# One decoder step on one core: the identity loaded first, dummy products, and the first product group ordered by terms and token halves

## The reference, cut to what matters

```python
def decoder_layer(h, p, attn_fn, conv_prev, lw):
    z = h @ lw['w_in']                       # (tokens x 1024) @ (1024 x 6400)
    q, k, v, c_b, c_c, c_h, g_a, g_c = jnp.split(z, IN_SPLITS, axis=-1)
    attn, new_k, new_v = attn_fn(q, k, v, lw['attn_sinks'])
    conv, new_conv = short_conv(c_c * c_h, conv_prev, lw['conv_w'])
    merged = (sigmoid(g_a) * (attn @ lw['w_attn_out'])
              + sigmoid(g_c) * (c_b * conv @ lw['w_conv_out']))
    h = layer_norm(DN_ALPHA * h + merged @ lw['w_o'], lw['ln1_g'], lw['ln1_b'])
    eidx, gw = route(x2, lw['w_router'], lw['router_bias'])
    ffn = swiglu(shared) + routed_experts(x2, eidx, gw, ...)
    ...
    return layer_norm(DN_ALPHA * h + ffn + ple, lw['ln2_g'], lw['ln2_b'])
```

## Time and profile before

| what | us |
|---|---|
| median of 3 runs (1264.17 to 1265.15) | 1264.87 |
| span of the profiled execution | 1265.4 |
| PE busy in the profiled execution | 1227.0 (97%) |
| first transpose starts | 7.09 |
| first product starts | 14.96 |
| group 1 starts | 28.32 |

### The profile page before, as it was taken

How to read it: one execution, slowest core, us unless ns; L and a number is a source line. 1 busy time by engine, 2 the same in 40 slices (tenths; PEclk the granted TensorE clock), 3 DMA queues, 4 the chain that set the end, 5 groups by cost and what they waited for, 6 DMA issues and landing times.

```text
span 1265.4 us, 23325 instructions
## 1 busy us (share of the span) xinstructions
PE 1227.0 (97%) x8776; PEld 974.0 (77%) x8777; DVE 497.9 (39%) x1103; ACT 306.3 (24%) x560; POOL 159.8 (13%) x228
## 2 busy tenths in 40 slices
PE   7999999999999999999899999999999999999977
PEld 7988879999999999998899666556555566666643
DVE  4456574423453433566886112112112221111137
ACT  4344453322221222316012111111111111111121
POOL 0200000000000000004336121111111121211100
PEclk9999999999999999999999999999999999999999
DMA  9312122322223232606337999999999999999986
GB/s 279 103 37 67 34 68 51 80 71 79 89 68 100 67 109 76 211 21 208 141 115 305 420 419 419 421 421 419 420 421 419 420 421 418 420 421 421 421 351 264
DMA packets 98656, 307.31 MB, mean 243 GB/s; under 512 B 11244, under 2 KB 62404, under 8 KB 72840
## 3 DMA queue, kind: packets, MB, share of 16 engines
q1 hardware_dynamic: 85332, 275.20, 56.2%
q0 software_dynamic: 12304, 28.60, 5.8%
q10 hardware_dynamic: 948, 2.50, 0.6%
HBM read 294.45 MB, written 26.94 MB: 254 GB/s over the span
## 4 chain that ended last, share of the span: by engine, by line
PE 55%; DMA 37%; DVE 5%; issue 1%; DVEq 1%; ACT 0%; SPq 0%; POOL 0%; ACTq 0%; POOLq 0%
DMA w_exp<-in_w_e_down_dram 35%; PE proj L1051 32%; PE proj L1243 4%; PE proj L1384 3%; PE att L1454 2%; PE proj L1473 2%; PE att L1165 2%; PE att L1127 1%; DMA fold<-expert_rows 1%; PE att L1252 1%; PE proj L1338 1%; PE att L1178 1%; PE proj L1368 1%; PE proj L1077 1%; DVE res L2124 1%
## 5 line engine op out<-in xcount | busy, mean ns | idle before, releaser
L1454 PE MATMUL att<-w_exp,xt 128*64 128x256 f32 x2560 | 286.3, 380 | 2.7 <-DMA w_exp<-in_w_e_up_dram 2.1
L1454 PEld LDWEIGHTS att<-w_exp,xt 128*64 128x64 f32 x2560 | 207.6, 137 | 90.2 <-issue 27.5
L1051 PE MATMUL proj<-h_hi,w_hi 128*128 128x288 f32 x768 | 171.1, 304 | 0.0
L1051 PE MATMUL proj<-h_hi,w_lo 128*128 128x288 f32 x768 | 164.2, 295 | 0.0
L1051 PE MATMUL proj<-h_lo,w_hi 128*128 128x288 f32 x768 | 164.0, 295 | 0.0
L1473 PE MATMUL proj<-w_exp,ht_e 128*64 128x512 f32 x640 | 146.1, 597 | 9.6 <-DMA w_exp<-in_w_e_down_dram 4.9
L1051 PEld LDWEIGHTS proj<-h_hi,w_hi 128*128 128x128 f32 x768 | 122.0, 188 | 16.2 <-issue 15.2
L1051 PEld LDWEIGHTS proj<-h_lo,w_hi 128*128 128x128 f32 x768 | 123.5, 188 | 0.0
L1051 PEld LDWEIGHTS proj<-h_hi,w_lo 128*128 128x128 f32 x768 | 123.4, 188 | 0.0
L468 DVE TENSOR_TENSOR w_lo<-w_raw,w_hi 128x2048 fp32r<-128x2048 f32 x33 | 75.6, 2291 | 91.9 <-ACT w_hi L458 86.8
L1473 PEld LDWEIGHTS proj<-w_exp,ht_e 128*64 128x64 f32 x640 | 50.4, 136 | 77.7 <-issue 76.0
(11 more groups left out here) (384 smaller groups left out, 1810.8 us busy)
## 6 DMA issues: line engine op xcount, KB each, us to landing
w_exp<-in_w_e_gate_dram SPq DMA_DIRECT2D x64, 1024.0 KB, 16.9
w_exp<-in_w_e_up_dram SPq DMA_DIRECT2D x64, 1024.0 KB, 17.0
w_exp<-in_w_e_down_dram SPq DMA_DIRECT2D x64, 1024.0 KB, 17.1
w_raw<-in_w_in_dram SPq DMA_DIRECT2D x21, 1024.0 KB
part<-expert_rows SPq DMA_DIRECT2D x8, 1536.0 KB, 21.2
w_raw<-in_w_in_dram SPq DMA_DIRECT2D x8, 512.0 KB
w_raw<-in_w_attn_out_dram SPq DMA_DIRECT2D x8, 512.0 KB
w_raw<-in_w_conv_out_dram SPq DMA_DIRECT2D x4, 1024.0 KB
```

The source lines that it names most:

```text
L1051: last = nc.tensor.matmul(proj[:, 2 * i + a, 0:HALF], lhs, x[:, c, a * HALF:(a + 1) * HALF], start=(c == 0 and n == 0), stop=(c == KC - 1 ...
L1454: last = nc.tensor.matmul(att[e * SLOT:(e + 1) * SLOT, m, 0:FF], xt[:, c, e * SLOT:(e + 1) * SLOT], weights[e][:, c, :], start=(c == 0), s ...
```

## The change

Four things change, all before group 1.

- ACT's queue issues `ident` first and tile 0 second.
- PE, as soon as `zeroed` is 2, does 11 products of the cleared head of `k_t` with itself (128 x 128, FP32) into bank 3 of `att`. Nothing reads them.
- In ACT's stream the split of group 0 stands behind the fourth copy, no longer behind the sixth.
- PE's products of group 0 are ordered by term and token half, and the last four quads stand between them: six quads, `hi*hi` of half 0 (16 products), four quads, `w_hi*h_lo` of half 0, `hi*hi` of half 1, `w_hi*h_lo` of half 1 (16 each), and last the 32 with `w_lo`. Count and sizes of transposes and products are as before.

```diff
+N_WARM = 11
         def _(act):
+            act.dma_start(ident[:, :], const1[:, 0:P]).then_inc(ld_x, 16)
             act.dma_start(x_tok[:, 0, :], xp[:, 0, :]).then_inc(tile_in[0], 16)
-            act.dma_start(ident[:, :], const1[:, 0:P]).then_inc(ld_x, 16)
...
-                if n == 5:
+                if n == 3:
                     split_hi(act, Step(0))
...
+            pe.wait_ge(zeroed, 2)
+            for _ in range(N_WARM):
+                nc.tensor.matmul(att[:, 3, 0:P], k_t[:, 0:WIN], k_t[:, 0:WIN], start=True, stop=True)
...
             pe.wait_ge(ld_x, 16)
+            token_quads(0, 6)
             pe.wait_ge(hi_done, 1)
+            pe.wait_ge(x_hi, 6)
+            for i in range(2):
+                first_products(0, 0, i)
+            token_quads(6, len(QUADS))
+            pe.wait_ge(x_lo, 6)
+            for i in range(2):
+                first_products(1, 0, i)
+            pe.wait_ge(x_hi, len(QUADS))
+            for i in range(2):
+                first_products(0, 1, i)
             pe.wait_ge(x_lo, len(QUADS))
+            for i in range(2):
+                first_products(1, 1, i)
             pe.wait_ge(w_ready, 1)
             for i in range(2):
+                for a in range(2):
+                    last = first_products(2, a, i)
                 last.then_inc(mm_ready[i], 1)
...
-            pe.wait_ge(zeroed, 2)
             pe.wait_ge(kv_tok_ready, 1)
```

More of the change, by code:

```diff
@@ L1060, in group @@
                         chunk(g, i, c, src_hi, src_lo)
-            pe.wait_ge(ld_x, 16)
[L1063 to L1078, removed]
-            pe.wait_ge(hi_done, 1)
[L1081 to L1085, removed]
+            pe.wait_ge(zeroed, 2)
@@ new lines, in _, with token_quads @@
+            for _ in range(N_WARM):
+                nc.tensor.matmul(att[:, 3, 0:P], k_t[:, 0:WIN], k_t[:, 0:WIN], start=True, stop=True)
+            def token_quads(first, last_n):
+                for n in range(first, last_n):
+                    t, c = QUADS[n]
+                    pe.wait_ge(tile_in[t], 16)
+                    if n >= 4:
+                        pe.wait_ge(x_lo, n - 3)
+                    w = ntok(t)
+                    for j in range(4):
+                        k = 4 * c + j
+                        last = nc.tensor.transpose(att[:, n % 4, j * P:j * P + w], x_tok[0:w, t, k * P:(k + 1) * P],
+                                                   ident[0:w, 0:w])
+                    last.then_inc(tr_x, 1)
@@ new lines, in first_products @@
+            def first_products(n, a, i):
+                w, x = ((w_hi, h_hi), (w_hi, h_lo), (w_lo, h_hi))[n]
+                for c in range(KC):
+                    lhs = w[:, 0, :].rearrange("p (c n) -> p c n", c=KC)[:, c, i * P:(i + 1) * P]
+                    last = nc.tensor.matmul(proj[:, 2 * i + a, 0:HALF], lhs, x[:, c, a * HALF:(a + 1) * HALF],
+                                            start=(c == 0 and n == 0), stop=(c == KC - 1 and n == 2))
+                return last
+            pe.wait_ge(ld_x, 16)
```

## The result

| | before | after |
|---|---|---|
| median us (range) | 1265.15 (1263.82 to 1267.24) | 1268.0 (1265.3 to 1270.02) |
| ratio, 95% interval | | 1.0017 (1.001 to 1.0024) |
| first product of group 0 | 14.96 | 13.57 |
| group 1 starts | 28.32 | 29.44 |

The ratio compares runs on the same chip; 0.17% of 1265 us is 2.1 us. The kernel became a little slower, by less than the 0.2% that counts as a difference here. The first product starts 1.39 us earlier and group 1 starts 1.12 us later: 2.5 us are lost between the two.

A forecast was written before the change was run, and what follows sets the result against it. PE's opening was taken to bound the kernel through group 1's start; +0.1 us for the new order plus 1.85 for low-clock products gave 1264.87 + 1.95 = 1266.8 us, range 1264.0 to 1268.0.

The forecast's parts named there:

- A: Main forecast: group 0's first products run at the low clock, +1.95 us (up to +2.75), 1266.8; chance 0.50.
- B: Rival: clock up and staying up when group 0's products start, despite 2 us idle; +0.1 to -0.7 us; chance 0.32.
- The bound and the lever: Opening before group 1: a microsecond PE wins or loses there moves the expert-weight loads and reaches the end nearly whole.
- The clock decides the sign: Before group 0's products: PE idles 2.0 us (2.9 if clock risen), then products cost 0.238 us instead of 0.133.
- Size of the loss: Group 0's first products: low clock for 4.2 to 6.0 us, costing 1.85 to 2.65 us.
- the fast branch: Opening's transposes at 0.11 us each: first product at 13.4 instead of 14.25, group 1 at 27.6, 0.7 us earlier.
- the uncovered transposes: Between group 0's products: sixteen transposes formerly hidden in ACT's split now cost 1.4 us.
- The dummies' length: Start of PE's stream: 11 dummy products start at 1.1, take 0.22 us apiece and end near 3.6, costing nothing.
- Tile 0's landing: Second load in ACT's queue: tile 0 lands at 6.6 us, between 5.2 and 7.0, without gain reaching the products.
- rival D: Opening: tile 0, now second, lands at 7.0 and PE starts as before; 1265 to 1266.8 us; chance 0.08.
- The stop for `w_lo`: PE's wait within group 0, 0.5 us before, goes: DVE ends `w_lo` at 21.7, its products come after 24.
- Rival C: Group 0's load shares DMA engines with tiles 0 to 3 and lands late; +3.7 us, 1268.6; chance 0.10.

The follow-up runs named there:

- e3: The changed kernel with eight dummy products added in PE's idle gap before the first products; median 1264.15 us, ratio 0.9996 to the kernel before.
- e7: The changed kernel with eight quads of transposes instead of six ahead of the first products; median 1264.77 us, ratio 0.9996 to the kernel before.
- e4: The changed kernel with all ten quads of transposes ahead of the first products; median 1264.94 us, ratio 0.9998 to the kernel before.
- e1: The changed kernel timed again, with nothing altered; median 1267.04 us, ratio 1.0013 to the kernel before.
- e8: The changed kernel with SP's load of group 0 held until the identity has landed; median 1271.54 us, ratio 1.0055 to the kernel before.
- e5: The changed kernel with ACT's first two loads as before, tile 0 then the identity; median 1266.78 us, ratio 1.0011 to the kernel before.
- e9: The kernel before with only the identity's load moved ahead of tile 0's; median 1265.55 us, ratio 0.9999 to the kernel before.
- e6: The kernel before with only the 11 dummy products added; median 1264.84 us, ratio 0.9997 to the kernel before.
- e2: The changed kernel without its 11 dummy products; median 1268.83 us, ratio 1.0029 to the kernel before.
- e10: The changed kernel with eight quads ahead, 14 dummies at the start and four behind the eighth quad; median 1263.25 us, ratio 0.9985 to the kernel before.

## Why the prediction was right, point by point

**The number.** Luck had a part in it. The forecast was 1266.8, and the median of 1268.0 lies on the upper end of the range. By the ratio, which compares on the same chip, the loss is 2.1 us against a forecast of 1.95; by the plain medians it is 2.85. The profiled execution's group 1, at 29.44, lies between the window of A (30.3 to 31.1) and that of B (27.6 to 28.5).

**The bound and the lever.** Right. A loss in the opening is carried on nearly whole: 1.12 at group 1 is 0.96 at 632 us. Through the expert stage it could be followed by medians only, since the late falls of the clock cover it in this pair of traces.

**The standing of the profiled execution.** I put it 0.5 above the median of the runs, taking the span for the time. With the 1.8 to 1.9 that lie between them it was 2.3 to 2.4 above three timed runs' 1264.87, so the sentence that a profile of after may show the same was wrong. It did not enter the sum, which is one of differences.

**The clock decides the sign.** Right in mechanism and place. PE idles before the first products, ACT ends the idle time (2.32 us; forecast 2.0, or 2.9 with the clock up), and the products start 0.24 apart, as forecast (0.238). e3 shows it by taking away nothing but the idle time; e7, which fills the idle time with real work, agrees. Without the slow products this execution's group 1 would have started at 29.44 - 1.36 = 28.08, 0.24 earlier than before.

**How it comes to be low.** This step was wrong in its story. I had the clock *not yet risen* at the products, because I let the dummies end at 3.6 and cut them off. They end at 6.19, and it rises at 6.32 (4.1 to 6.4 us in eight of the nine profiles with dummies, 10.65 in e4). It then *falls*, in the gap before the products. So the sentence in rival B, that an idle stretch of 2 us does not make it fall, is what failed in these executions; B's other half, that the dummies suffice to raise it, held in all of them but e4's.

**Size of the loss.** Sixteen products take 3.71 in place of 2.35: 1.36 us, where I had 1.85 to 2.65. The clock was low for 3.42 us (13.14 to 16.56), of which 2.99 lay on the products, not the 4.2 to 6.0 read off two later places. (The step from fast to slow was priced at 0.105 a product; 0.09 x 288/256 is 0.101, and 0.107 was measured, 0.240 against 0.133.) Against that the transposes ran fast, and the first product came at 13.57, near the 13.4 of the fast branch. Together: 13.57 + 12.8 + 1.6 for the uncovered transposes + 1.36 = 29.3, seen 29.44. The 2.5 us lost between the first product and group 1 are these 1.36 and 1.6, less the 0.5 of the stop that went. A's 30.3 to 31.1 was met by e1's execution (30.56), with its second fall, and not by after's. Both errors of size point the same way, so that this execution is 0.8 better at group 1 than forecast (+1.12, not +1.95). Executions like e1's, with a second fall, are worse (+2.24). The measured +2.1 lies between these two, nearer to e1's; the forecast of +1.95 is close to it as a median of such executions, not as a description of the one profiled.

**The dummies' length.** Mis-sized by two. I priced a product at one transpose, 0.22. The 11 instructions make 22 passes in the trace, 0.213 us apart (1.13 to 6.19): an FP32 product that is no transpose shows as two. The earlier trace rows has it too (x6 for the three products of the tables), and I did not use it. It was harmless in the change, since tile 0 landed only at 7.35; in e8 tile 0 landed at 5.03, and PE turned to it only at 5.98, behind the last dummy pass.

**Tile 0's landing.** I took 6.6 between 5.2 and 7.0; it was 7.35, above my upper bound. The reason was right: the second DMA of ACT's queue waits for SP's load (e5, e8, e9). The Trainium skill (DMA: Bandwidth & Descriptors, Queues, rings and completion order) has the engines go round-robin between queues; by that rule alone tile 0 should follow the identity at once, and the landing of 5.03 in e8 against 7.35 disagrees with it for this first megabyte. Thus most of rival D came true, and it was worth nothing, as its sum said: tile 1 and ACT stand in between. Tiles 1 and 2 landed at 8.83 and 10.11, near the forecast 8.8 and 10.4.

**Small terms.** The stop for `w_lo` went: DVE had it at 22.52, PE wanted it from 25.20. The uncovered transposes cost 1.6 (forecast 1.4). Rival C's late load did not come: group 0 landed at 8.24, where it had landed at 10.19 before and at 10.20 in e5, with tile 0 first. The swap brought it in earlier, not later. e8 shows what lateness would have cost.

**What each part does, in medians.** Swap: nothing (e5, e9). Dummies: -0.4 on the old order, not told from none (e6), and -2.0 on the new (e1 against e2). The new order without cover for ACT's split: the loss, which e3 and e7 take back. The earlier place of ACT's split has no run of its own. **Still open**: whether e2's slower executions fall before the products, and by how much an execution's moment of rise alone moves the time. Medians also spread by more than one trace tells: e3 has group 1 at 28.94 and is faster than e6 with 27.73.

## What to carry to other kernels

Moving work behind a wait to start something earlier takes away what kept PE busy in that wait; count the idle time that is left there, for here a gap of 2.3 us in front of dense products cost 1.36 us, as much as the earlier start (1.39) had won, and the work that was moved out of the wait cost another 1.6. What warm-up products win can be lost again in a gap behind them (in e1 the clock fell at 8.23, in e6 at 7.51), so put such products, or real work as in e7, into the gap itself. And of two profiles look first at milestones and at the clock along the whole run, since one fall that has nothing to do with the edit can turn the sign of a difference of 1 us.

## What the runs showed of the hardware that I had not expected

- The clock fell during or soon after idle stretches of 1.57 us (e3, 8.87), 1.73 (e7, 9.09), 1.92 (e6, 7.51), 1.95 (e5, 14.80), 2.00 and 2.27 (e1, 8.23 and 15.06) and 2.32 (after, 13.14), and did not after 1.30 (after, before tile 0), 1.38 (e10), 1.61 (e5, before tile 0), 1.66 (e4), 1.84 (e2) or, in before, 1.89. Length of idle alone does not decide. The Trainium skill (TensorE: Matmul & The Clock Gate, What's actually happening) says that one and the same kernel meets its transition to the higher level at differing places from run to run; the two executions of the changed kernel agree, with the first rise at 6.32 in one and at 4.82 in the other.
- The low stretches of the opening measured 3.4 us in after (13.14 to 16.56), in e1 (15.06 to 18.47) and in e3 (8.87 to 12.28), and 6.8 us in e8 (13.25 to 20.07), where PE did nothing until 16.53.
- A small DMA second in ACT's queue takes 5.8 us to land, and 2.5 as the first. The same place costs 512 KB 6.1 us, and 3.9 when SP's megabyte is held back (e8).
